# A first stage that starts behind its tokens, and an expert choice that counts: a Trainium2 kernel of two transformer blocks, changed at its start and at the router

## What is computed

```
# layer 0
hn = rms_norm(h, mix_norm[0])
q, k, v, r, lr_f, lr_b = split(hn @ w_in)            # "gla": gated linear attention
h = h + gla(...) ;  h = h + swiglu(rms_norm(h, ffn_norm[0]), dense weights)
# layer 1
h = h + sliding_window_attention(rms_norm(h, mix_norm[1]))
t = rms_norm(h, ffn_norm[1])
logits = t @ router                                   # 256 x 8
top_val, top_idx = top_k(logits, 2)                   # the first of equals wins
combine = sum(one_hot(top_idx) * softmax(top_val))
for e in range(8): out += combine[:, e] * swiglu(t, w_gate[e], w_up[e], w_down[e])
# then a second block of two attention layers and a final norm
```

## Time and profile before

| | |
|---|---|
| median of 3 runs | 1700.71 us (1699.63 to 1700.82) |
| the profiled execution | 1700.05 us, its span 1698.2 us |
| PE busy | 1588.2 us, 94% of the span |
| DVE, ACT, POOL busy | 1209.3, 1038.1, 66.8 us |
| chain that ended last | PE 80%, ACT 8%, DVE 8%, issue 3% |
| first product of the q projection | starts at 22.12 us |
| first product of expert 0 | starts at 476.77 us |

### The profile page before, as it was taken

One profiled execution on the slowest core, in us unless ns is written; L12 is line 12 of the kernel. 1 busy time (PEld: TensorE's weight loads), 2 busy tenths in 40 slices (PEclk: granted clock), 3 DMA queues, 4 the chain that ended last, 5 costly groups with the idle time before them and its releaser, 6 DMA issues.

```text
span 1698.2 us, 21565 instructions
## 1 busy us (share of the span) xinstructions
PE 1588.2 (94%) x8601; PEld 1327.4 (78%) x8601; DVE 1209.3 (71%) x1383; ACT 1038.1 (61%) x1242; POOL 66.8 (4%) x78
## 2 busy tenths in 40 slices
PE   5998999998799999999999999999998997889977
PEld 5867888788678888888888888888877886778865
DVE  3665555368578888888888888888885566555655
ACT  4645444357467777677777767676776547455463
POOL 0000000023000000000000000000000200012000
PEclk9999999999899999999999999999998999999989
DMA  7422655552369999899999999999897642346401
GB/s 254 149 100 99 204 190 176 194 198 71 107 225 346 373 327 351 310 387 360 340 328 315 404 318 363 332 333 389 311 326 185 115 126 76 71 84 139 131 25 38
DMA packets 133081, 389.32 MB, mean 229 GB/s; under 512 B 8694, under 2 KB 14266, under 8 KB 132844
## 3 DMA queue, kind: packets, MB, share of 16 engines
q1 hardware_dynamic: 132692, 387.15, 66.9%
q10 hardware_dynamic: 280, 0.70, 0.1%
HBM read 386.78 MB, written 1.05 MB: 228 GB/s over the span
## 4 chain that ended last, share of the span: by engine, by line
PE 80%; ACT 8%; DVE 8%; issue 3%; DMA 0%; POOL 0%; ACTq 0%; DVEq 0%; POOLq 0%
PE psum L361 24%; PE psum L363 24%; PE psum L362 23%; DVE wlo L194 4%; ACT whi L184 3%; PE psum L1585 1%; PE psum L1637 1%; ACT Ss L1242 1%; PE psum L2330 1%; ACT hh L1697 0%; PE psum L440 0%; PE psum L2211 0%; PE psum L367 0%; PE psum L1666 0%; PE psum L2165 0%
## 5 line engine op out<-in xcount | busy, mean ns | idle before, releaser
L194 DVE TENSOR_TENSOR wlo<-raw,whi 128x2048 fp32r<-128x2048 f32 (+1 forms) x286 | 630.2, 2214 | 225.0 <-ACT whi L184 224.0
L184 ACT ACTIVATE whi<-raw 128x2048 fp32r<-128x2048 f32 (+1 forms) x286 | 526.0, 1847 | 234.7 <-PE psum L363 234.5
L361 PE MATMUL psum<-whi,xh 128*128 128x512 f32 (+1 forms) x1232 | 477.2, 387 | 16.1 <-DVE xl L2683 10.1
L363 PE MATMUL psum<-whi,xl 128*128 128x512 f32 (+1 forms) x1232 | 467.6, 380 | 0.0
L362 PE MATMUL psum<-wlo,xh 128*128 128x512 f32 (+1 forms) x1232 | 466.1, 378 | 0.0
L361 PEld LDWEIGHTS psum<-whi,xh 128*128 128x128 f32 x1232 | 233.2, 189 | 70.0 <-issue 13.6
L363 PEld LDWEIGHTS psum<-whi,xl 128*128 128x128 f32 x1232 | 232.9, 189 | 47.3
L362 PEld LDWEIGHTS psum<-wlo,xh 128*128 128x128 f32 x1232 | 233.4, 189 | 44.1 <-issue 0.2
L194 DVE TENSOR_TENSOR wlo<-raw_more,whi 128x2048 fp32r<-128x2048 f32 (+1 forms) x94 | 204.0, 2177 | 39.0 <-ACT whi L184 38.2
L184 ACT ACTIVATE whi<-raw_more 128x2048 fp32r<-128x2048 f32 (+1 forms) x94 | 171.4, 1827 | 53.0 <-PE psum L363 53.0
L361 PE MATMUL psum<-xh,whi 128*128 128x256 f32 (+2 forms) x552 | 165.1, 299 | 16.9 <-DVE wlo L194 15.3
(11 more groups left out here) (391 smaller groups left out, 1595.8 us busy)
## 6 DMA issues: line engine op xcount, KB each, us to landing
raw<-in_moe_w_down_dram SPq DMA_DIRECT2D x58, 1024.0 KB, 7.7
raw<-in_moe_w_gate_dram SPq DMA_DIRECT2D x43, 1024.0 KB, 6.5
raw<-in_moe_w_up_dram SPq DMA_DIRECT2D x41, 1024.0 KB, 5.7
raw_more<-in_moe_w_down_dram SPq DMA_DIRECT2D x30, 1024.0 KB, 7.5
raw<-in_w_in_dram SPq DMA_DIRECT2D x28, 1024.0 KB, 8.0
raw_more<-in_moe_w_up_dram SPq DMA_DIRECT2D x23, 1024.0 KB, 5.9
raw_more<-in_moe_w_gate_dram SPq DMA_DIRECT2D x21, 1024.0 KB, 6.7
raw<-in_moe_w_up_dram SPq DMA_DIRECT2D x23, 768.0 KB, 5.8
```

Of the source, the lines that this page charges most:

```text
L184: act.e.activation(self.whi[:, i % self.ns, 0:kt * n], self.place[self.slots[i]][:, 0:kt * n], ACT.Copy, scale=1.0).then_inc(self.s_hi)
L194: dve.e.tensor_tensor(self.wlo[:, i % self.ns, 0:kt * n], self.place[self.slots[i]][:, 0:kt * n], self.whi[:, i % self.ns, 0:kt * n].bitca ...
L361: pe.e.matmul(o, lh, rh, start=start, stop=False)
L363: return pe.e.matmul(o, ll, rh, start=False, stop=stop)
```

## The change

At the start:

- SP issues weight piece 0 right behind the tokens, then the nine small transfers, then pieces 1 to 3. The constants come in two transfers, and the tokens have a semaphore for each half. ACT loads the table of the root at the very start.
- ACT squares tile 0 of the tokens, DVE tile 1 (a new `tensor_tensor_reduce`). `pc` is copied behind the scaling.
- The tokens are turned into four banks (4 to 7) in place of six, so step k waits for the low part of step k - 4.
- POOL makes the high and low part of piece 0 in four slices of 512 columns (`first_to`), and PE takes the first q piece slice by slice, with all four column groups for each slice.
- The zeroing of `wg` and `sco` on POOL no longer waits.

At the router:

- ACT copies part 7 of `xf` ahead of both `xnh`; DVE makes `xnl` behind the selection matrix.
- The two rounds of maxima are replaced: `above` holds for each pair of experts whether the one is greater, or equal and earlier; its sum is the expert's place, and places 0 and 1 are chosen. The slots stay one higher, and `places` compares with `base + 1`.
- PE counts with fp32r operands (POOL copies the triangle and the ones, `c3r`).
- The first gathering uses seven banks: first all high products of steps 0 to 6, then all low ones, then step 7. ACT waits for the exponential alone ahead of the table of silu; `route.ends` is waited for at the copy of `PT`.
- On ACT, DVE and PE the body of the branch is written behind the rest of the list, and the list goes on right behind the compare.

```diff
+    def first_to(self, pool):
+        _, kt, n = self.pieces[0]
+        raw = self.place[self.slots[0]]
+        for k in range(kt):
+            c = slice(k * n, (k + 1) * n)
+            pool.wait_ge((self.landed[self.slots[0]], 16))
+            pool.e.tensor_copy(self.whi[:, 0, c], raw[:, c]).then_inc(self.s_first)
+            pool.wait_ge((self.s_first, 2 * k + 1))
+            pool.e.tensor_tensor(self.wlo[:, 0, c], raw[:, c], self.whi[:, 0, c].bitcast(F32),
+                                 ALU.subtract).then_inc(self.s_first)
...
-            sp.wait_ge((ld_prm, 16 * len(rows)))
-            for i in range(RAW):
+                sp.e.dma_start(H[:, t, :], I["x"][0, t * 128:(t + 1) * 128, :]).then_inc(ld_x[t], 16)
+            W.fetch(sp, 0)
+            for at, r in zip(pcol, rows):
+                sp.wait_ge((s_prm0, 1))
+                sp.e.dma_start(prm[at:at + r.shape[0], :], r).then_inc(ld_prm, 16)
+            for i in range(1, RAW):
                 W.fetch(sp, i)
...
+            wh, wl = W.views(0)
+            for k in range(4):
+                for j, (c, m) in enumerate(G4):
+                    pe.wait_ge(W.first(k), x(k), *([(s_pc, 1)] if j == 0 else []))
+                    ins = mm3(pe, psum[:, j, 0:T], wh[:, k, c:c + m], wl[:, k, c:c + m], xh[:, k, 0:T], xl[:, k, 0:T], k == 0, False)
+            ins.then_inc(W.s_passed)
...
-            squares(act, "gla", 0, [(H[:, j, :], 128) for j in range(2)], xn[:, :, :].rearrange("p a b -> p (a b)"),
-                    (ld_x, 32))
+            squares(act, "gla", 0, [(H[:, 0, :], 128)], xn[:, 0, :], (ld_x[0], 16))
+            act.wait_ge(s_table.at("gla", -2))
...
+            Start.copied(act)
+            high_by_gain(act, "gla", T, G_MIX[0], banks=TB4)
...
+            dve.e.tensor_tensor_reduce(xn[:, 1, :], H[:, 1, :], H[:, 1, :], 1.0, 0.0, ALU.mult, ALU.add,
+                                       st[:, 1:2]).then_inc(n_dve.end("gla", "sq"))
...
+            dve.e.tensor_tensor(above[:, :, :, 0:8], of_each, to_each, ALU.is_gt).then_inc(r.end("greater"))
+            dve.e.tensor_tensor(same[:, :, :, :], of_each, to_each, ALU.is_equal).then_inc(r.end("equal"))
+            dve.wait_ge(r.at("equal"), (ld_c3, 32))
+            dve.e.tensor_tensor(above[:, :, :, 8:16], same[:, :, :, :],
+                                c3[:, 256:320].rearrange("p (a b) -> p a b", a=8).unsqueeze(1).to_broadcast([128, 2, 8, 8]),
+                                ALU.mult).then_inc(r.end("earlier"))
+            dve.e.tensor_reduce(place[:, :, :], above[:, :, :, :], AX, ALU.add).then_inc(r.end("place"))
+            dve.e.tensor_scalar(ch[:, :, :], place[:, :, :], 2.0, None, ALU.is_lt).then_inc(r.end("chosen"))
...
+            def gather_first():
+                pe.wait_ge(s_P.at(0), (xn_hi, 2))
+                for k in range(7):
+                    for j in range(2):
+                        gathered(0, k, j, xnh)
+                for k in range(7):
+                    for j in range(2):
+                        pe.wait_ge((xn_lo, j + 1))
+                        ins = gathered(0, k, j, xnl)
+                    ins.then_inc(g_acc.end(0, k))
+                pe.wait_ge(g_lo.at(0, 0))
...
+    def where_over_aside(p, aside, after):
+        home = nc.cur_bb
+        p.e.br_ne(flag_of(p), 0, aside, after)
+        nc.switch_bb(after)
+        return met_by(p), home
...
+    with nc.bb("over_pe", parent=home):
+        second_launch(inside, over_pe)
+        nc.tensor.br("experts_pe")
```

More of the change, by code:

```diff
@@ L133, with __init__ @@
 class Weights:
-    def __init__(self, sem, name, pieces, slots, ns, whi, wlo, place):
+    def __init__(self, sem, name, pieces, slots, ns, whi, wlo, place, apart=0):
         self.pieces, self.slots, self.ns, self.whi, self.wlo, self.place = pieces, slots, ns, whi, wlo, place
@@ L317, in body @@
     slots += [tail[i % RAW] for i in range(len(pieces) - moe1)]
-    W = Weights(sem, "w", pieces, slots, NS, whi, wlo, {i: raw[:, i, :] for i in range(RAW)})
+    W = Weights(sem, "w", pieces, slots, NS, whi, wlo, {i: raw[:, i, :] for i in range(RAW)}, 1)
     NORMS = ["gla", "head1", "head0", "dense", "swa", "moe", "meta0", "b0", "b1", "meta1", "end1", "end0"]
@@ L1356, in make_route @@
         n_hi, n_lo = sem("xn_high"), sem("xn_low")
-        r = steps("route", ("logits",), *[(1, x) for x in best], ("rest",), *[(2, x) for x in best], ("chosen",),
-                  ("diff",), ("sum",), ("inverse",), ("second",), ("count",), ("w1",), ("w2",), ("slots",), ("cw",), ("slot",))
+        s_c3 = sem("c3_copied")
+        r = steps("route", *[(x,) for x in ("logits", "greater", "equal", "earlier", "place", "chosen", "best", "hot1", "rest",
+                                            "count", "slots", "next", "diff", "sum", "inverse", "second", "hot2", "w1", "w2",
+                                            "cw")])
         def xf_at(k):
@@ L1421, in dve, with b8 @@
             copied_dve(dve, 6)
+            lg, hot1, hot2, rest = tp[:, 0], tp[:, 1], tp[:, 3], tp[:, 2]
+            of_each, to_each = (lg.unsqueeze(n).to_broadcast([128, 2, 8, 8]) for n in (2, 3))
+            sl2 = slot[:, :, :].rearrange("p a b -> p (a b)")
+            def b8(t):
+                return t.unsqueeze(2).to_broadcast([128, 2, 8])
+            dve.wait_ge((s_logits, 1), n_dve.at("moe", "rstd"))
+            dve.e.tensor_tensor(lg, psum[:, 0:2, 0:8], b8(st[:, 0:2]), ALU.mult).then_inc(r.end("logits"))
@@ new lines, in dve @@
+            dve.e.scalar_tensor_tensor(rest, hot1, -3e38, lg, ALU.mult, ALU.add).then_inc(r.end("rest"))
+            dve.wait_ge((s_pos, 1))
+            dve.e.tensor_reduce(cnt[:, 0:1], psum[:, 4, 0:8], AX, ALU.max).then_inc(r.end("count"))
+            dve.wait_ge(r.at("count"))
+            dve.e.tensor_scalar(flag[:, :], cnt[:, 0:1], 128.0, None, ALU.is_gt).then_inc(s_flag)
+            dve.wait_ge((s_pos, 2))
+            dve.e.scalar_tensor_tensor(sl2, psum[:, 3, 0:16], 1.0, ch[:, :, :].rearrange("p a b -> p (a b)").bitcast(F32), ALU.add,
+                                       ALU.mult).then_inc(r.end("slots"))
@@ L1422, in dve @@
+            dve.wait_ge(r.at("slots"), (ld_c3, 32))
+            places(dve, Pm0, 0, 0, 2).then_inc(moe_marks[0].end(0))
+            dve.e.tensor_reduce(sm[:, 1], rest, AX, ALU.max).then_inc(r.end("next"))
+            dve.wait_ge(r.at("next"), r.at("best"))
+            dve.e.tensor_tensor(sm[:, 2], sm[:, 1], sm[:, 0], ALU.subtract).then_inc(r.end("diff"))
             for j in range(2):
-                dve.wait_ge((n_hi, j + 1), n_dve.at("moe", "rstd"))
+                dve.wait_ge((n_hi, j + 1))
@@ L1785, in body, with flag_of @@
     more.close()
-    def where_over(p, stage):
+    def flag_of(p):
         p.wait_ge((s_flag, 1))
@@ L2921, in _ @@
         Start.pool(pool)
-        for stage in (gla, swa):
+        for stage in (gla, swa, route):
             stage.pool(pool)
```

243 lines of the change are left out of this document (131 added, 112 removed).

## The result

The changed kernel takes 1690.99 us (median of 4 runs, 1689.64 to 1692.01) against 1700.62 in the runs beside it (1699.63 to 1700.82): a ratio of 0.9938, with an interval of 0.9924 to 0.9952. That is 9.6 us, not the 14.7 of the prediction; the median lies 0.5 us above the range of 1682.5 to 1690.5, and its interval, 1687.7 to 1692.5, reaches well into that range. The profiled execution took 1692.01, the slowest of the four; its span is 1690.5, 7.7 us shorter than the span before. What follows accounts for this one execution.

What follows compares the result with a forecast made beforehand. The prediction held that PE paces the kernel, so delays before its work are paid in full; 7.1 us at the start plus 7.6 at the router give 14.7, for a median of 1686.0 us, range 1682.5 to 1690.5.

Steps and rivals of the forecast that it cites:

- The start: At the kernel's start: first q product at 15.0 us in place of 22.12, a gain of 7.1 us.
- The small transfers: At the start: the nine small transfers land 0.8 us behind weight piece 0, at 11.0 us (bounds 10.2 and 11.8).
- the bounds (up to 9.5): At the start: gain 6.3 to 7.9 us, up to 9.5 if the clock rises earlier as turns run straight into products.
- POOL's slices: At the start: POOL makes each slice of piece 0 in 1.85 us and would gate PE only from 2.65.
- rival D: Behind q, at the gates: the start's gain is given back; half lost 1689.6 us, all lost 1693.1; chance 0.07.
- Rival B: At the start: POOL's slices, stretched beside DVE to 2.8 us, set the pace; gain 3.7, time 1689.4 us; chance 0.17.
- C: At the start: POOL's slices take 5.87 us each as in the worst rows; time 1701.6 us, slower; chance 0.03.
- The router: From the logits to the experts: expert 0 at 469.1 us in place of 476.77, a gain of 7.6 us.
- rival A: At the router: the branch still fetches code, so expert 0 comes 3.0 us later; time 1689.0 us; chance 0.11.
- 7.1 + 7.6 = 14.7 us: Whole kernel: the gains of start and router simply add, taking the profiled 1700.05 us to 1685.4.

Runs made afterwards that it cites:

- e1: The kernel before with the changes of the start alone, router and branch as before; 1694.38 us, ratio 0.9955.
- e4: The changed kernel with the body of the router's branch back inside the lists; 1691.45 us, ratio 0.9932.
- e5: The changed kernel with eight unused columns (32 bytes a partition) put back into the table of constants; 1687.94 us, ratio 0.991.
- e7: The changed kernel with eight unread products filling PE's idle 2.08 us ahead of `gla vr3`; 1687.66 us, ratio 0.9916.
- e9: The changed kernel with 16 unused columns (64 bytes a partition) in the table of constants; single run, 1689.24 us.
- e10: The changed kernel with 24 unused columns (96 bytes a partition) in the table of constants; single run, 1686.31 us.
- e6: The changed kernel with the nine small transfers issued by ACT between the halves of the constants, as before the change; 1689.57 us, ratio 0.9925.
- e11: The changed kernel with the small transfers between the halves of the constants on ACT, and a semaphore of its own for the first half; 1689.3 us, ratio 0.992.
- e12: The changed kernel with the edits of e5, e7 and e11 together; 1684.94 us, ratio 0.9894.
- e2: The kernel before with the router's counting and gathering of the change, start and inline branch as before; 1697.76 us, ratio 0.9972.
- e3: The kernel before with only the branch's body written behind the lists of ACT, DVE and PE; 1699.87 us, ratio 0.9978.

## Why the prediction was right in sign and 5 us short in size

**The start: forecast 7.1, measured 7.1,** with two terms off that cancel, and in an execution that lies at the low end: with the same start the traces of e1, e4, e5, e7, e9 and e10 give 7.3 to 8.8 us. The exact hit is luck; the mechanism is not. The small transfers landed at 11.9, not 11.0: 1.5 us behind piece 0 (POOL, which waits for it, starts at 10.43) where I took 0.8 from how far they had landed behind the tokens, and q started at 15.64 instead of 15.0. The pace gave it back: the products come at full pace from 2.1 us behind the start of q on, where it had been 3.4. I had this in the bounds (up to 9.5) and not in the sum. Tokens were ready at 10.7 (forecast 10.2), POOL's slices took 1.92 us each (1.85). The shift did not go through whole: 0.4 us of it (0.7 in e6, e11 and e12) is gone at the wait ahead of `gla vr3`, in every trace with POOL's slices and in none without; that is rival D in small. Rival B and C are out, but e11 shows where B begins: as soon as DVE's low parts reach the slices.

**The router: forecast 7.6, measured 8.1.** Step by step, on the scale of before (4.4 us later): logits' end 455.8 (forecast 455.9), chosen 1.7 us behind the logits' start (1.7), slots at 458.9 (459.0), first gathering 460.0 (460.15), DVE free at 463.6 (464.6) and its first low part at 464.5, behind ACT's high part, expert 0 468.7 (469.1). The branch takes 0.09 us (0.1), so rival A is out; e4 puts its worth at 3.1 us on PE and 2.4 at expert 0. The two halves do not simply add: the changed router with the inline branch gains 5.8 us in e4 and 4.8 in e2, where the slow stretch across the router is 13.7 us long and not 10.2.

**The step that failed is the sum itself:** "7.1 + 7.6 = 14.7 us" assumes that all other work takes as long as before. It also priced the dropped columns at nothing by not naming them. In its place the profiled execution showed 7.5 us lost:

- 1.5 to 1.8 us over the experts, because the tensors behind the table, `hh` and `hl` among them, moved by 32 bytes. Shown by e5, e9 and e10. It stood in the diff, as the dropped columns.
- 4.6 us of two stretches at the lower clock. The one near 89 (1.6 us) comes and goes with the same kernel text and the same idle time. The one near 1362 (3.0 us) does not come and go: it is in all ten traces that have the changed start and the changed router together (the changed kernel and e4 to e12, 3.4 or 6.8 us long, 1.5 or 3.0 us lost) and in none of before, e1 and e2, one trace each; e3 has 3.4 us of it. So it may well be a cost of the change as it stands. The idle stretch ahead of it is 2.26 us now and 2.27 before, so a longer wait is not the reason. What decides is open.
- 0.4 us of a longer wait for DVE ahead of `gla vr3`, 2.08 in place of 1.64, since the start changed. Why it is longer was not looked into.
- 0.7 us between 103 and 429, 0.3 of it between 132 and 140, where every profile has a slow stretch, and 0.3 between 300 and 349, where none has. e1 and e12 lose 0.5 and 0.3 in all, and e2, with the start of before, 0.8: it is not the start's. Why is open.

The last 0.2 lie behind 1387. The median execution falls short of the forecast by 5.1 us, not 7.0 as the profiled one; of that the runs show 1.8 as the place's, and the rest is not divided.

With the place mended, no fall near 89 and half of the one near 1362, e12 comes to 1684.9, about where the prediction had put the change alone (1686.0).

## What to carry to other kernels

A sum of gains holds only if the rest keeps its pace. Lay one engine's regular instructions of both traces side by side, and each step in the difference names a place to look at. When an edit drops or adds a small tensor, ask what lies behind it in SBUF, and look at the mean time of the products that read it. When a transfer is moved out of a queue's way, look at what shares its semaphore: in e6 the wait only passed to the next one, and a semaphore of its own brought the first turn of the tokens from 12.35 to 9.42 us. And before a difference of 1 to 2 us at one place is put down to an edit, look at the same place in other traces in which that place was not edited: e9 has e11's gain without e11's edit.

## What the runs showed of the hardware that I had not expected

- Products of 128x512 that read `hh` or `hl` are 1 to 4 ns slower each when these tensors lie 32 bytes lower (391 or 392 ns against 395 for `wlo,hh`), over 924 such products in 700 us, 1.9 us in all by the groups' busy time. Of four places, 32 bytes apart, the first and third are slow and the second and fourth fast.
- PE's granted clock differs from one execution to the next at the same work: the kernel before ran from 1699.52 to 1709.64 us in 21 runs taken together, at a mean granted clock of 0.979 to 0.972. A difference of 2 to 5 us needs the stretches of clock beside it.
- Nine small transfers behind 1 MB on the same queue landed some 1.5 us behind it; on ACT's queue they had landed 0.8 behind the tokens. And how long q's first products run slow differs among executions of one start, from 0.2 to 2.7 us, though the turns run straight into them in all.
